# Modulation products in full f32 on four column groups, riding between other chunks, and the first z product moved to the first attention

## The reference, cut to what matters

```
for l in range(DEPTH):                                   # 2 layers
    mod_lat = silu_c @ w_mod[l] + b_mod[l]               # 3072 values: shift, scale, gate
    mod_ctx = silu_cc @ w_mod[l] + b_mod[l]
    h_lat = rms_norm(x, norm_g) * (1.0 + scale) + shift
    h_ctx = rms_norm(ctx, norm_g) * (1.0 + scale_c) + shift_c
    ... = split_cols(h @ w_in)                           # queries, keys, values, z, gm
    terms.append(sigmoid(gr) * ((y * silu(zr)) @ w_branch[r]))   # r = 0, 1, 2
    x = x + gate * ((terms[0] + terms[1] + terms[2]) @ w_out)
```

## Time and profile before

| | |
|---|---|
| time before, median of 3 runs | 2510.17 us (2509.56 to 2511.52) |
| the profiled execution's own time | 2509.31 us |
| its span | 2507.5 us |
| TensorE, VectorE, ScalarE busy | 2432.3, 1499.0, 1238.2 us |
| TensorE's mean granted clock | 0.992 of full |
| read from HBM | 312.55 MB |

### The profile page before, as it was taken

One profiled execution on the slowest core, in us unless ns is written; L12 is line 12 of the kernel. 1 busy time (PEld: TensorE's weight loads), 2 busy tenths in 40 slices (PEclk: granted clock), 3 DMA queues, 4 the chain that ended last, 5 costly groups with the idle time before them and its releaser, 6 DMA issues.

```text
span 2507.5 us, 33363 instructions
## 1 busy us (share of the span) xinstructions
PE 2432.3 (97%) x12709; PEld 2011.0 (80%) x12709; DVE 1499.0 (60%) x2512; ACT 1238.2 (49%) x2323; POOL 30.0 (1%) x54
## 2 busy tenths in 40 slices
PE   6999999999999999899999999999999998999999
PEld 3978788778888887688887888878888887888887
DVE  6563344684458545665647677665669846556565
ACT  6652322663237433564336545464556555554643
POOL 2000000000000000000000000000000000000000
PEclk8999999999999999999999999999999999999999
DMA  7412343113430223343621541555555661655554
GB/s 226 137 51 84 118 126 93 51 60 100 119 85 10 76 84 118 95 145 101 185 84 43 168 126 51 175 189 175 183 172 173 193 187 42 205 177 175 185 168 134
DMA packets 164766, 317.86 MB, mean 127 GB/s; under 512 B 10454, under 2 KB 22608, under 8 KB 164096
## 3 DMA queue, kind: packets, MB, share of 16 engines
q1 hardware_dynamic: 161552, 303.67, 39.4%
q0 software_dynamic: 3056, 12.06, 1.7%
HBM read 312.55 MB, written 3.15 MB: 126 GB/s over the span
## 4 chain that ended last, share of the span: by engine, by line
PE 86%; DVE 8%; ACT 3%; issue 2%; DMA 1%; SPq 0%; DVEq 0%; ACTq 0%
PE bank L820 24%; PE bank L822 23%; PE bank L821 23%; PE bank L839 6%; PE bank L956 5%; DVE w_low_part L1623 2%; DVE neg_max L2020 1%; PE bank L918 1%; PE bank L929 1%; ACT w_high_part L1158 1%; DMA w_raw<-in_w_mod_dram 1%; PE bank L1017 1%; PE bank L935 0%; PE bank L932 0%; PE bank L1084 0%
## 5 line engine op out<-in xcount | busy, mean ns | idle before, releaser
L1623 DVE TENSOR_TENSOR w_low_part<-w_raw,w_high_part 128x1024 fp32r<-128x1024 f32 (+3 forms) x592 | 693.7, 1189 | 583.9 <-ACT w_high_part L1158 580.6
L1158 ACT ACTIVATE w_high_part<-w_raw 128x1024 fp32r<-128x1024 f32 (+3 forms) x592 | 601.4, 1033 | 718.5 <-PE bank L822 705.8
L820 PE MATMUL bank<-w_high_part,h_high 128*128 128x512 f32 (+3 forms) x2128 | 816.6, 384 | 11.9 <-DVE h_low L1913 7.3
L822 PE MATMUL bank<-w_high_part,h_low 128*128 128x512 f32 (+3 forms) x2128 | 808.0, 380 | 0.0
L821 PE MATMUL bank<-w_low_part,h_high 128*128 128x512 f32 (+3 forms) x2128 | 807.2, 379 | 0.0
L820 PEld LDWEIGHTS bank<-w_high_part,h_high 128*128 128x128 f32 x2128 | 401.5, 189 | 87.7 <-issue 10.2
L822 PEld LDWEIGHTS bank<-w_high_part,h_low 128*128 128x128 f32 x2128 | 401.1, 188 | 74.7
L821 PEld LDWEIGHTS bank<-w_low_part,h_high 128*128 128x128 f32 x2128 | 401.7, 189 | 71.3
L1449 ACT ACTIVATE stage<-bank,neg_max 128x512 f32<-128x512 f32 (+1 forms) x240 | 147.2, 616 | 130.8 <-DVE neg_max L2020 72.9
L839 PE MATMUL bank<-ident,stage 128*128 128x128 f32 (+1 forms) x1112 | 167.7, 278 | 12.3 <-DVE probs_turned L2036 3.0
L839 PEld LDWEIGHTS bank<-ident,stage 128*128 128x128 f32 (+1 forms) x1112 | 127.0, 140 | 64.7 <-issue 46.0
(11 more groups left out here) (292 smaller groups left out, 2449.1 us busy)
## 6 DMA issues: line engine op xcount, KB each, us to landing
w_raw<-in_w_in_dram SPq DMA_DIRECT2D x160, 512.0 KB, 3.6
w_raw<-in_a_w_in_dram SPq DMA_DIRECT2D x96, 512.0 KB, 4.1
w_raw<-in_b_w_in_dram SPq DMA_DIRECT2D x80, 512.0 KB, 4.5
w_raw<-in_w_mod_dram SPq DMA_DIRECT2D x48, 512.0 KB, 4.1
w_raw<-in_w_branch_dram SPq DMA_DIRECT2D x48, 512.0 KB, 4.3
w_raw<-in_a_w_out_dram SPq DMA_DIRECT2D x32, 512.0 KB, 4.7
w_raw<-in_c_w_in_dram SPq DMA_DIRECT2D x32, 512.0 KB, 3.9
w_raw<-in_w_out_dram SPq DMA_DIRECT2D x16, 512.0 KB, 4.0
```

Source lines behind the costliest of these rows:

```text
L820: pe.matmul(o, high, wh, start=(k == 0), stop=False)
L822: mm = pe.matmul(o, low, wh, start=False, stop=(k == u.kt - 1))
L1158: nc.scalar.activation(WH[:, c % PART_SLOTS, 0:kt, 0:width], RAW[:, c % RAW_SLOTS, 0:kt, 0:width], ACT.Copy).then_inc(*S.up("w_high", c))
L1623: v.tensor_tensor(WL[:, s, 0:kt, 0:width], RAW[:, r, 0:kt, 0:width], WH[:, s, 0:kt, 0:width].bitcast(F32), ALU.subtract).then_inc(*S.up("w ...
```

## The change

The modulation weights are no longer split. `ride` multiplies the raw chunk in f32 with the two condition columns (`COND`), in four matmuls of 256 columns: k piece kk and column half `half` go to partitions 32 x (2 kk + half), so each of the four has a column group of the array to itself, and all four are accumulated side by side in one bank over the four chunks. The raw slot becomes free when TensorE has used it. The sums over kk are made in `modulation`: four f32 matmuls of a 98-row piece of `MODROW` with a selection matrix `SEL`.

In layer 0 the modulation units (0, 4), (0, 5) and (1, 0) to (1, 5) become riders: after each chunk of the unit that carries one, TensorE does one chunk of the rider. They use the "out" banks. `to_split` lists the chunks that are split, and the part slots count in it. (0, 0) to (0, 3) stay at the start, each with a "wide" bank that is cleared first.

The unit z(l, 0, 0) moves from behind the first attention to its opening, in both layers: the first two items are scored after its chunk 0, the last queries are turned before its last chunk, and its sigmoid times z is kept in `ACC`, with which `outputs` multiplies. The tail of the first attention moves to z(l, 0, 1).

Smaller parts: the norm of layer 0 is put ahead of all modulation units, with x fetched after two chunks; in both layers ScalarE scales the context tiles and VectorE the latent ones; GpSimd's small loads wait for the use of chunk 10; after the unit (0, 3) two chunks are split, and the next two at k = 2 of `turn_h`.

```diff
 def plan():
+    def place(u, rider=None):
+        if rider:
+            u.rider = modulation_unit(*rider)
+        u.pfirst = len(to_split)
+        for n, chunk in enumerate(u.chunks):
+            u.at.append(len(chunks))
+            if u.kind != "mod":
+                to_split.append(len(chunks))
+            chunks.append(chunk)
+            if rider:
+                u.rider.at.append(len(chunks))
+                chunks.append(u.rider.chunks[n])
+        u.plast = len(to_split) - 1
...
     steps.append(("condition",))
+    steps.append(("norm", 0, ALL_TILES))
...
             steps.append(("norm", l, ALL_TILES))
-            mod(1, 3)
-            mod(1, 4)
             steps.append(("turn_h", l, 0))
...
-        mod(l, 4 if l == 0 else 5)
...
         steps.append(("attend_first", l, 0, qt))
-        if l == 0:
-            mod(0, 5)
-            with_turn(pend.pop(0))
-        else:
-            steps.append(("turn_qk", pend.pop(0)))
+        gemm("z", ("z", l, 0, 0), qt, ("h", l), w_in, D, OFF_Z, 512, j=0, l=l, r=0, head=(l, 0, qt))
+        with_turn(pend.pop(0))
...
+            riders = {("z", 0, 0): (0, 4), ("gm", 0, 0): (0, 5), ("t", 0, 0): (1, 0), ("t", 0, 1): (1, 1),
+                      ("z", 1, 1): (1, 2), ("gm", 1, 0): (1, 3), ("t", 1, 0): (1, 4),
+                      ("t", 1, 1): (1, 5)} if l == 0 else {}
+            if r:
+                gemm("z", ("z", l, r, 0), qt, ("h", l), w_in, D, OFF_Z + D * r, 512, j=0, l=l, r=r, tail=(l, r, qt))
+            gemm("z", ("z", l, r, 1), qt, ("h", l), w_in, D, OFF_Z + D * r + 512, 512, j=1, l=l, r=r,
+                 tail=None if r else (l, r, qt), rider=riders.get(("z", r, 1 if r else 0)))
...
-        if l == 0:
-            mod(1, 0)
...
 SyncE
-                    sp.wait_ge(*S.at("w_low", c - RAW_SLOTS))
+                    free = "w_low" if c - RAW_SLOTS in part_of else "w_used"
+                    sp.wait_ge(*S.at(free, c - RAW_SLOTS))
...
-            for c in range(RAW_SLOTS):
+            for c in range(2):
                 weights(c)
             for t in ALL_TILES:
                 x = dram["ctx"] if t in CTX_TILES else dram["x"]
                 sp.dma_start(X[:, t, :], ...)
-                if t % 2:
-                    weights(RAW_SLOTS + t - 1)
-                    weights(RAW_SLOTS + t)
-            for c in range(RAW_SLOTS + 4, len(chunks)):
+            for c in range(2, len(chunks)):
                 weights(c)
...
 GpSimd
-            pool.wait_ge(*S.at("w_low", 11))
+            pool.wait_ge(*S.at("w_used", 10))
...
 TensorE
+                    if u.rider:
+                        ride(u.rider, n)
...
+            def ride(u, n, pool="out"):
+                c = u.at[n]
+                slot, k0 = c % RAW_SLOTS, u.chunks[n][1]
+                pe.wait_ge(S.sem(f"w_landed{slot}"), 16 * (c // RAW_SLOTS + 1))
+                once(left_ready(u.left, k0))
+                if pool == "wide":
+                    once(S.at("banks_cleared"))
+                if n == 0:
+                    rider_bank[0] = take(pool, (u.key, 0))
+                b = rider_bank[0]
+                last = n == len(u.chunks) - 1
+                for kk in range(KT):
+                    for half in range(2):
+                        a = 32 * (2 * kk + half)
+                        mm = pe.matmul(banks[b][a:a + 2, 0:256], COND[:, k0 + kk, :],
+                                       RAW[:, slot, kk, 256 * half:256 * half + 256], start=(n == 0), stop=last)
...
             def modulation(l, j):
                 once(S.emptied((("mod", l, j), 0)))
-                turn(("turn", "mod", l, j), [(MODROW[:, P * f:P * f + P], 4 * f) for f in range(4)],
-                     "wide" if l == 0 and j < 4 else "turn")
+                once(S.at("selection"))
+                b = take("wide" if l == 0 and j < 4 else "turn", ("turn", "mod", l, j))
+                for f in range(4):
+                    mm = pe.matmul(banks[b][:, 2 * f:2 * f + 2], MODROW[0:98, P * (f % 2):P * (f % 2) + P],
+                                   SEL[0:98, f // 2, :], start=True, stop=True)
+                mm.then_inc(*fills(b))
...
 ScalarE
+            def take_modulation(key):
+                act.wait_ge(*S.filled((key, 0)))
+                if mods:
+                    act.wait_ge(*S.filled(("turn",) + mods[-1]))
+                mods.append(key)
+                nc.scalar.copy(MODROW[0:98, :], ps((key, 0))[0:98, 0:256]).then_inc(*S.empties((key, 0)))
...
+                    elif u.kind == "z" and u.key[2:] == (0, 0):
+                        nc.scalar.activation(ACC[:, t, 0:512], src[:, :],
+                                             ACT.Sigmoid).then_inc(*S.up("z_sigmoid", key))
...
             def norm(l, tiles):
+                if l == 0:
+                    for t in tiles:
+                        act.wait_ge(S.sem(f"x{t}_landed"), 16)
+                        last = nc.scalar.activation(XN[:, t, :], X[:, t, :], ACT.Square, accum_out=STAT[:, 0, t:t + 1])
...
+                if l < 2:
+                    act.wait_ge(*S.at("x_inverse", l))
+                    for half in range(2):
+                        cols = slice(512 * half, 512 * half + 512)
+                        for t in CTX_TILES:
+                            nc.scalar.activation(XN[:, t, cols], X[:, t, cols], ACT.Copy,
+                                                 scale=STAT[:, 2, t:t + 1]).then_inc(*S.up("normed_ctx", (l, t, half)))
...
             def turn_h(l, half):
                 for k in range(KD) if half else ():
+                    if l == 0 and k == 2:
+                        prepare(PART_SLOTS)
...
 VectorE
                     for half in range(2):
                         cols = slice(512 * half, 512 * half + 512)
-                        for t in tiles:
+                        for t in LAT_TILES:
...
             def outputs(l, r, t, g):
+                if (r, g) == (0, 0):
+                    for h in range(n):
+                        f = slice(w * h, w * h + w)
+                        ins = v.scalar_tensor_tensor(out=Y[:, t, f], in0=src[:, h, :], scalar=RL[:, t % 2, 0, h:h + 1],
+                                                     in1=ACC[:, t, f], op0=ALU.mult, op1=ALU.mult)
```

More of the change, by code:

```diff
@@ L137, in __init__, with modulation_unit, gemm @@
         self.more = more
-        self.first = None
+        self.at = []
+        self.rider = None
+        self.pfirst = self.plast = None
 def plan():
-    steps, chunks = [], []
-    def gemm(*args, **more):
-        u = Unit(*args, **more)
-        u.first = len(chunks)
-        chunks.extend(u.chunks)
-        u.last = len(chunks) - 1
+    steps, chunks, to_split = [], [], []
+    def modulation_unit(l, j):
+        return Unit("mod", ("mod", l, j), (0,), ("cond",), ("w_mod", l), D, 512 * j, 512)
+    def gemm(*args, rider=None, **more):
+        return place(Unit(*args, **more), rider)
+    def place(u, rider=None):
[11 more added lines that the diff above has]
+        u.plast = len(to_split) - 1
         steps.append(("gemm", u, None))
         modulation_due()
+        if rider:
+            owed.append(rider)
         return u
@@ L351, in plan @@
     steps.append(("store",))
-    return steps, chunks
+    return steps, chunks, to_split
 HEADS = {0: MH, 1: DH, 2: SH}
@@ L385, in program @@
         S = Signals(nc, ctx, known)
-        steps, chunks = plan()
+        steps, chunks, to_split = plan()
         units = [s[1] for s in steps if s[0] == "gemm"]
@@ L486, in program @@
         RSTD = place("x_rstd", [P, 2])
+        SEL = place("mod_select", [P, 2, 2])
         STAT = place("stats", [P, 3, 32])
@@ L786, in gemm @@
                 open_banks = {}
+                if u.kind == "mod":
+                    for n in range(len(u.chunks)):
+                        while late and late[0][0] <= n:
+                            turn(*late.pop(0)[1])
+                        ride(u, n, "wide")
+                    return
                 for n, (src, k0, kt, col, width) in enumerate(u.chunks):
@@ L812, in gemm @@
                             high, low = left_high_low(u.left, k, t)
-                            o = banks[b][0:4 if u.left[0] == "cond" else P, 0:width]
+                            o = banks[b][:, 0:width]
                             wh, wl = WH[:, slot, kk, 0:width], WL[:, slot, kk, 0:width]
-                            if low is None:
-                                pe.matmul(o, high, wh, start=(k == 0), stop=False)
-                                mm = pe.matmul(o, high, wl, start=False, stop=(k == u.kt - 1))
-                                continue
                             pe.matmul(o, high, wh, start=(k == 0), stop=False)
@@ L864, in turn_h @@
                 pieces = [(("turn", "h", l, k), [(XN[:, t, P * k:P * k + P], P * t) for t in ALL_TILES], "turn4",
-                           [("normed", (l, t, k // 4)) for t in ALL_TILES]) for k in range(KD)]
```

(17 more changed lines are left out.)

149 lines of the change are left out of this document (68 added, 81 removed).

## The result

The changed kernel takes 2532.5 us (median of 4 runs, 2531.09 to 2536.42) against 2510.85 for the kernel before on the same chip: ratio 1.0089, 95% interval 1.0071 to 1.0106. It is slower by 22 us, where I had forecast no change that can be told. The profiled execution took 2533.31 us with a span of 2531.5, so the profile has to explain +24.0 us of span.

A forecast was written before the change was run, and what follows sets the result against it. TensorE, busy 2432.3 of 2507.5 us, was taken as the bound. Stream +18.2, start -8.3, between layers -7.0 and first attention -3.0 summed to -0.1 us: 2510.1 us predicted, range 2487 to 2535.

The forecast's parts named there:

- the ring runs dry: Rival: chunks and riders share five raw slots; 1 us missing at each of eight units, 2518 us; chance 0.08 with the clock.
- riders of 1.82 us: Rival: f32 products never run side by side on column groups, each rider costs 1.82 us, 2535 us; chance 0.20.
- The riders: Layer 0 stream: 32 modulation chunks behind other products, five steps plus exit, 1.2 us each, 38.4 us in all.
- all four groups at once: Rival: a rider's four column groups work simultaneously, 0.53 us per rider, 2488.7 us; chance 0.12.
- The 0.1 us that I had charged for leaving the groups: Each rider's end: the next whole-array product starts about 0.1 us later, included in 1.2 us per rider.
- The row turns: Stream: turning a modulation row by four f32 matmuls, eight instructions, takes 0.9 us, 8 times, 7.2 us.
- The wait at the tail: First attention's tail in layer 0: rider (0, 4) holds an output bank, so TensorE waits 2.0 us, once.
- What was removed: Running stream: six modulation units and their row turns go, 29.4 us less.
- The start: Before layer 0: unsplit chunks land sooner, first product at 40.5 us, gain 8.3 us (3 to 12).
- the 3.5 us from that last product to the scaling: Start: from the last modulation product to the column scaling 3.5 us, filled by two row turns and a copy; before 5.2.
- Between the layers: Gap before layer 1: chunks go, first product 9.5 us sooner, 2.5 charged for lower clock, net -7.0 (-10 to -4).
- The first attention: Its opening in both layers: the moved z product covers the turning of queries, net -3.0 us (-4 to +1).

The follow-up runs named there:

- experiment 1: Changed kernel, but where consecutive units both carry riders, ScalarE and VectorE split the next unit's third chunk after emptying this unit's banks: 2500.54 us, ratio 0.9970.
- experiment 2: Changed kernel with the same eight riders on other units, leaving two neighbouring pairs with riders instead of four: 2517.06 us, ratio 1.0037.
- Experiment 3: experiment 1 with all four products of each rider's or start chunk on one column group, modulation rows thus wrong: 2540.25 us.
- experiment 5: experiment 1 with the eight riders moved on, none on the unit holding the first attention's tail: 2502.20 us.
- Experiment 6: experiment 1 with GpSimd's small loads waiting for the use of chunk 15 and no longer chunk 10: 2497.15 us, ratio 0.9952.
- Experiment 4: experiment 1 with the first gate product (z) back behind the first attention in both layers: 2502.24 us.

## Why the prediction was wrong

**The step that failed is the rival "the ring runs dry".** It was worked out for a steady row of riders, "a pair lasts 24 x 0.23 + 1.2 = 6.7 us; with the 1.19 of splitting a fetch has over 10 us", and priced at 1 us at each of eight units, chance 0.08 with the clock. Inside a unit that is right: no wait for a chunk stands there. At the change of unit it isn't. There the third chunk's slot is freed by the unit's last instruction, and the wait for it stands ahead of the emptying in the program of two engines. I looked at when the ring delivers to TensorE, and not at what is queued behind the engine that waits for the ring. The price is 7 us idle and 2 us of clock at four places, 36 us, as experiments 1 and 2 show from two sides. That 2532.5 us lies inside the range is luck: its upper end was made of riders of 1.82 us, and they were short.

**The riders** were mis-sized. The mechanism of the less likely rival "all four groups at once" was right, and its price of 0.53 us was too low. Predicted 1.2 us each for 32, from the argument that a group's second half waits for its first and the next group with it. The changed kernel's timeline:

```profile
237.55 0.39 PE L831 MATMUL bank<-w_high_part,h_low 128*128 128x512 f32 x1
237.87 0.61 PE L858 MATMUL bank<-w_raw,cond 128*2 128x256 f32 x8
238.41 0.50 PE L829 MATMUL bank<-w_high_part,h_high 128*128 128x512 f32 x1
238.75 0.40 PE L830 MATMUL bank<-w_low_part,h_high 128*128 128x512 f32 x1
```

The rider starts 0.32 us after the main product (0.23 would be the step without it), the next main product 0.54 us after the rider, and the one behind that 0.34 us later and not 0.23. With 0.02 us more in the next few steps a rider costs 0.77 us: a chunk with one lasts 6.21 us, and 5.44 in the kernel before. That is 24.5 us for 32 and not 38.4. The 0.1 us that I had charged for leaving the groups is there three times: on the way in, in the 0.54 for two steps of 0.215, and in the step behind. Experiment 3 gives the other bound: 1.82 us to the next start in one group, the 1.82 that I had.

I had cited 2.38x for three column groups from the Trainium skill, page "TensorE: Matmul & The Clock Gate", section on packing small matmuls. The same section gives a span model, which I had passed over: one product's duration, and some 4 ns for each further tile. By it four f32 products would take 0.43 + 3 x 0.004 = 0.44 us, an estimate, and with 0.1 us for the way out 0.54. The trace agrees: 0.54 to the next start. The first halves of the four products start 6 to 7 ns apart, and so do the second halves, 0.195 us behind them. The estimate leaves out the slower steps before and behind.

**The row turns** cost 0.9 us each, as predicted: the products' starts fall back by 1.68 us where a rider and a turn come together, 0.77 + 0.91. **The wait at the tail** was 2.1 us (2.0), for the bank that the rider held, as experiment 5 shows. **What was removed** covered something that I had missed: the modulation units (0, 4) and (1, 5) stood ahead of the first key/value up-projection while VectorE split the turned latent rows (c_low). Now TensorE waits 1.2 us there in each layer, 2.4 us in the waits after.

**The start**: predicted 40.5 us for the first product, measured 44.61, so -4.2 and not -8.3. The landing was right, small loads included: the last modulation product came at 34.63 us for 34.5. So were the 2.53 us from scaling to product. The term that failed is the 3.5 us from that last product to the scaling, which took 7.4. The row turns ran at the lower clock, and ScalarE waited 2.96 us for the layer's second weight chunk, which I had put ahead of the scaling without asking when it lands. Experiment 6 has no such wait, takes 4.5 us there and gets 40.76; there the first of the two row turns takes 1.09 us and not 1.87. What the wait and the turns cost each was not separated. It is the pattern of the four stalls once more: a wait for a transfer, ahead of work that TensorE needs.

**Between the layers**: predicted 9.5 us sooner less 2.5 for the clock; measured 10.6 sooner, of which the first 60 products give back 0.8 (28.7 and then 29.5 us behind).

**The first attention**: predicted -3.0 for both layers, and more came. In layer 1 the products gain 2.5 us (25.7 behind before it, 23.2 after). In layer 0 they are 7.4 us ahead at the last product before it, and the scores behind the opening are 5.2 behind. The z unit put in between is 21.8 us and the unit (0, 5) taken out 5.4, so the opening itself gained 3.7 us, in which the kernel before had a low stretch of 3.4 us (at 139 us). Experiment 4 shows 3.2 us of gain there against a kernel with the z unit moved back. So -6.2.

The sum with what was measured: riders 24.5, turns 7.3, tail 2.1, removed -29.4, c_low +2.4, the pairs +36.1, start -4.2, between the layers -10.6, attention -6.2: +22.0 of +24.0 us. Of the rest 0.7 us lies in the first products of layer 0, which fall into a longer stretch of low clock than before, and 0.7 behind 1200 us, where the low stretches of the two traces differ. The last 0.6 us stay unassigned. Such stretches, of 0.5 to 2 us each, come and go between executions.

## What to carry to other kernels

When a new consumer shares a ring of buffers, write out which slot each entry gets at the change of stage and which instruction frees it, and then look in every engine's program at what stands behind the wait for that entry. A wait for a transfer that stands ahead of the emptying of banks turns a late prefetch into a stall of the engine that computes. The profile names the last link of such a chain; follow the line's own engine back until something waits for a DMA or for the stalled engine itself. And the price of a wait of 7 us on TensorE was 9: low clock came with it.

## What the runs showed of the hardware

Four f32 products of 256 columns on four column groups take the time of one: eight halves end within 0.61 us, and the next product starts 0.54 us after the first; on one group it is 1.89 and 1.82 us. The two halves of one group's product do not hold up the other groups: four halves start within 0.02 us, and the other four 0.195 us later. Around them the change from and to whole-array products costs some 0.1 us on the way in and 0.2 on the way out, half of it in the step behind the next product. The Trainium skill's page "TensorEngine Tiling (Array Packing)", key properties, says that changing the mode drains the engine, and by these rows no more than that is lost.

Full DMA engines moved 300 GB/s in a stretch of 4 us without GpSimd's small loads (experiment 6), and 166 and 203 GB/s in the same stretch with them (experiment 1 and the changed kernel).
